# Two norms made one, and a value projection started before the head norms, in a 256-token transformer kernel

## The reference, cut to what matters

```python
def _rms(x, g):
    xf = x.astype(F32)
    y = xf * lax.rsqrt(jnp.mean(xf * xf, axis=-1, keepdims=True) + RMS_EPS)
    return (y * g.astype(F32)).astype(x.dtype)
...
return rmsnorm(x, final_g)                # end of first_block
...
h = x                                     # second_block
xn = _rms(h, norm_mix[i])
qa, ka, va, qb, kb, vb = jnp.split(xn @ w_in, [...], axis=-1)
oa = _moba(_rms(_heads(qa, MOBA_HEADS), qn_a), _rms(_heads(ka, MOBA_HEADS), kn_a), _heads(va, MOBA_HEADS), ...)
ob = _dilated(_rms(_heads(qb, DIL_HEADS), qn_b), _rms(_heads(kb, DIL_HEADS), kn_b), _heads(vb, DIL_HEADS), ...)
h = h + (concatenate([oa, ob]) @ w_out)
```

## Time and profile before

| what | us |
|---|---|
| median of 3 runs (lowest, highest) | 2900.24 (2899.81, 2912.12) |
| the profiled execution: its own time | 2900.88 |
| the profiled execution: span, first to last instruction | 2898.9 |
| TensorE matmul busy | 2687.6 (93%) |
| TensorE weight load busy | 2263.1 (78%) |
| VectorE busy | 1563.7 (54%) |
| ScalarE busy | 1320.6 (46%) |
| GpSimd busy | 22.0 (1%) |
| mean granted TensorE clock | 0.953 |

### The profile page before, as it was taken

How to read it: one execution, slowest core, us unless ns; L and a number is a source line. 1 busy time by engine, 2 the same in 40 slices (tenths; PEclk the granted TensorE clock), 3 DMA queues, 4 the chain that set the end, 5 groups by cost and what they waited for, 6 DMA issues and landing times. The chain is left out here.

```text
span 2898.9 us, 40646 instructions
## 1 busy us (share of the span) xinstructions
PE 2687.6 (93%) x15617; PEld 2263.1 (78%) x15617; DVE 1563.7 (54%) x2281; ACT 1320.6 (46%) x2001; POOL 22.0 (1%) x34
## 2 busy tenths in 40 slices
PE   6999998998899999899999798997899998889998
PEld 3788786875688877688876657997669997768998
DVE  7444434885644433644323565545757656556655
ACT  6444323464544422544312354544446544445644
POOL 0000000000000000000000000000000001000000
PEclk9999998999999999999999899999999999779999
DMA  6444532201344422344322202544215544302544
GB/s 244 174 159 163 191 138 73 97 20 44 119 170 153 165 102 101 122 168 155 131 90 100 103 1 81 181 174 162 102 59 188 181 178 162 128 11 73 188 174 145
DMA packets 52721, 374.81 MB, mean 129 GB/s; under 512 B 5823, under 2 KB 7035, under 8 KB 8737
## 3 DMA queue, kind: packets, MB, share of 16 engines
q1 hardware_dynamic: 50288, 360.73, 34.7%
q0 software_dynamic: 1920, 12.27, 1.2%
q10 hardware_dynamic: 432, 0.73, 0.1%
HBM read 372.55 MB, written 7.39 MB: 131 GB/s over the span
## 5 line engine op out<-in xcount | busy, mean ns | idle before, releaser
L1092 DVE TENSOR_TENSOR wlo<-raw,whi 128x1024 fp32r<-128x1024 f32 x666 | 799.6, 1222 | 823.0 <-ACT whi L657 821.9
L657 ACT ACTIVATE whi<-raw 128x1024 fp32r<-128x1024 f32 x666 | 684.7, 1053 | 867.6 <-PE acc L1586 781.5
L1584 PE MATMUL acc<-hhi,whi 128*128 128x256 f32 (+1 forms) x2800 | 939.7, 336 | 53.9 <-DVE hlo L1176 36.2
L1585 PE MATMUL acc<-hlo,whi 128*128 128x256 f32 (+1 forms) x2800 | 934.0, 334 | 0.0
L1586 PE MATMUL acc<-hhi,wlo 128*128 128x256 f32 (+1 forms) x2800 | 933.0, 333 | 0.0
L1584 PEld LDWEIGHTS acc<-hhi,whi 128*128 128x128 f32 x2800 | 536.4, 192 | 117.0 <-issue 61.9
L1586 PEld LDWEIGHTS acc<-hhi,wlo 128*128 128x128 f32 x2800 | 536.4, 192 | 50.8
L1585 PEld LDWEIGHTS acc<-hlo,whi 128*128 128x128 f32 x2800 | 536.8, 192 | 48.8 <-issue 0.2
L1584 PE MATMUL acc<-ghi,whi 128*128 128x512 f32 (+1 forms) x1056 | 364.0, 345 | 22.5 <-DVE glo L1249 15.1
L1585 PE MATMUL acc<-glo,whi 128*128 128x512 f32 (+1 forms) x1056 | 362.8, 344 | 0.0
L1586 PE MATMUL acc<-ghi,wlo 128*128 128x512 f32 (+1 forms) x1056 | 362.5, 343 | 0.0
(11 more groups left out here) (245 smaller groups left out, 2584.6 us busy)
## 6 DMA issues: line engine op xcount, KB each, us to landing
raw<-in_slabs SPq DMA_DIRECT2D x333, 1024.0 KB, 4.8
ada_raw<-in_slabs SPq DMA_DIRECT2D x8, 1024.0 KB, 22.8
skew_dram<-lines_dram POOLq DMA_DIRECT2D x1, 6144.0 KB, 24.9
bt<-skew_dram POOLq DMA_DIRECT2D x4, 1024.0 KB, 6.5
x<-in_x_in SPq DMA_DIRECT2D x1, 2048.0 KB, 18.0
out<-x SPq DMA_DIRECT2D x1, 1024.0 KB, 4.8
rope<-in_rope POOLq DMA_DIRECT2D x1, 512.0 KB, 4.0
mask<-in_mask POOLq DMA_DIRECT2D x1, 512.0 KB, 4.7
```

The source lines that it names most:

```text
L657: nc.scalar.activation(whi[:, n % 2, cols], raw_of(n, cols), ACT.Copy).then_inc(ready, 1)
L1092: nc.vector.tensor_tensor(wlo[:, n % 2, cols], raw_of(n, cols), whi[:, n % 2, cols].bitcast(F32), ALU.subtract).then_inc(low, 1)
L1584: nc.tensor.matmul(out, w[0], xx[0], start=first, stop=False)
L1585: nc.tensor.matmul(out, w[0], xx[1], start=False, stop=False)
```

## The change

Four things are changed, all between the last `down` of the first block and the end of the first decoder attention.

1. The final norm is no stage of its own. With `both` set, ScalarE squares each pair of tiles twice: once scaled by the root of eps (columns 0 to 255 of `sq`), once scaled by `final_g` (two instructions of 128x256, columns 256 to 511). VectorE's adds to `prod` are 128x1024 in place of 128x512. TensorE sums both parts into one bank in four matmuls, which gives the mean square of the normed stream times its norm, and then makes two more for the plain sum (`x_summed`). One root and one reciprocal give the scale of the mixer norm of the final norm, and `two_gains` holds the product of both gains. The loops over the halves of `down` are written out, and the root's table is loaded by `preload` behind the last `hi`.
2. `x` itself gets its final norm later: the second root goes to `rs[:, 256:512]` (`x_root`), VectorE takes its reciprocal in unit 11, and the eight products, each followed by a wait for itself, in units 12 to 19.
3. TensorE does value slab 0 and half of value slab 1 before it waits for `att_ready`; the other half stands behind the first three scores, and a wait for ScalarE's copy of slab 1 behind that. Slab 1 has a bank of its own, the one in which the units' transposes lie. Slabs 2 and 3 go, in 11 units each, into units 2 to 12 and 13 to 23, one and two steps in turn.
4. ScalarE's and VectorE's half-slabs stand elsewhere: `hi` of the first free slab ahead of the units and `lo` in units 0 and 2, the others `hi` in 4, 7, 14, 17, 25, 28 and `lo` in 5, 8, 15, 18, 26, 29. The copies of slabs 2 and 3 stand at the start of units 14 and 24.

```diff
@@ -166,9 +167,10 @@
             st += ffn_stages(1, S, mod=2)
-    st += [Stage("norm", T=S, how="final")]
+    st[-1].both = True
     for layer in range(2):
         st += [Stage("norm", T=S, how="gain", gain=VCOL["norm_mix"] + DT * layer)]
+        st[-1].both = layer == 0
         if layer == 0:
@@ -516,9 +522,17 @@
+def value_bank(c):
+
+    return acc[:, 1, 1, :] if c == 1 else v_bank
+
 def turn_bank(st, u):
...
     return acc[:, 1, 1, :] if st.what == "ab" else acc[:, u % 2, 1, :]
+
+def gain_of(st, c):
+
+    return two_gains[:, c:c + 1] if st.both else vec[:, st.gain + c:st.gain + c + 1]
@@ -593,6 +606,8 @@
         pool.wait_ge(rs_ready, st.rs0 + 1)
+        if st.both:
+            pool.wait_ge(x_summed, 1)
         for k in range(1, st.items, 2):
@@ -690,8 +705,12 @@
         act.wait_ge(sum_done, st.sum0 + (1 if st.summed else DT))
-        nc.scalar.activation(rs[:, 0:st.T], sums[:, 0:st.T], ACT.Sqrt, bias=eps[:, 0:1], scale=1.0 / D)\
-            .then_inc(std_ready, 1)
+        nc.scalar.activation(rs[:, 0:st.T], sums[:, 0:st.T], ACT.Sqrt,
+                             bias=(eps_sq if st.both else eps)[:, 0:1], scale=1.0 / D).then_inc(std_ready, 1)
+        if st.both:
+            act.wait_ge(x_summed, 1)
+            nc.scalar.activation(rs[:, S:2 * S], B[2][:, 0:S], ACT.Sqrt, bias=eps[:, 0:1],
+                                 scale=1.0 / (D * ROOT_EPS * ROOT_EPS)).then_inc(x_root, 1)
@@ -772,17 +791,22 @@
                         act.wait_ge(sq_added, st.add0 + c + 1 + 2 * i)
-                        nc.scalar.activation(sq[:, :, 0:st.T], x[:, bass.ds(2 * c + 4 * i, 2), 0:st.T],
-                                             ACT.Square).then_inc(sq_ready, 1)
+                        ins = nc.scalar.activation(sq[:, :, 0:st.T], x[:, bass.ds(2 * c + 4 * i, 2), 0:st.T],
+                                                   ACT.Square, scale=ROOT_EPS if st.both else 1.0)
+                        for t in range(2) if st.both else ():
+                            g = VCOL["final_g"] + 2 * c + t + 4 * i
+                            ins = nc.scalar.activation(sq[:, t, S:2 * S], x[:, 2 * c + t + 4 * i, 0:S],
+                                                       ACT.Square, scale=vec[:, g:g + 1])
+                        ins.then_inc(sq_ready, 1)
                     hi(st.n0 + 2 + ks * c + kk, i, 2 * ks)
-        if st.feeds:
+        if st.feeds or st.both:
             half(0)
...
                 half(i)
-        if st.feeds:
+        if st.feeds or st.both:
             preload(ACT.Sqrt)
@@ -796,8 +820,6 @@
             root(st)
-        if st.how == "final":
-            return
         for k in range(st.items):
@@ -1036,16 +1057,19 @@
             value_rows(0)
+            hi(st.n0 + 2)
         for u in range(LEAD):
             exps(u)
+        if ab:
+            value_rows(1)
         for u in range(UNITS):
-            if ab and u % 8 == 0 and u:
-                value_rows(u // 8)
+            if ab and u in (14, 24):
+                value_rows(2 + u // 24)
             copied(u)
...
                 exps(u + LEAD)
-            if ab and u % 8 in (2, 5):
-                hi(st.n0 + u // 8 + 2, halves=(u % 8 // 5,))
+            if ab and u in (4, 7, 14, 17, 25, 28):
+                hi(st.n0 + 3 + u // 10, halves=((u % 10 + u // 20) // 7,))
             if u % 4 == 1 and u > 4:
@@ -1255,8 +1278,9 @@
+        wide = 2 * S if st.both else st.T
         dve.wait_ge(g_lo, st.g0 + 1)
-        step.done(nc.vector.memset(prod[:, :, 0:st.T], 0.0))
+        step.done(nc.vector.memset(prod[:, :, 0:wide], 0.0))
         if st.kind == "pw2":
@@ -1296,11 +1320,11 @@
                         dve.wait_ge(sq_added, st.add0 + c + 1 + 2 * i)
-                        nc.vector.tensor_tensor(prod[:, :, 0:st.T], prod[:, :, 0:st.T], sq[:, :, 0:st.T],
+                        nc.vector.tensor_tensor(prod[:, :, 0:wide], prod[:, :, 0:wide], sq[:, :, 0:wide],
                                                 ALU.add).then_inc(sq_added, 1)
...
-        if st.feeds:
+        if st.feeds or st.both:
             half(0)
@@ -1542,8 +1566,17 @@
                 biased(u + LEAD)
-            if st.what == "ab" and u % 8 in (3, 6):
-                lo(st.n0 + u // 8 + 2, halves=(u % 8 // 6,))
+            if st.what == "ab" and u == 11:
+                dve.wait_ge(x_root, 1)
+                step.done(nc.vector.reciprocal(rs[:, S:2 * S], rs[:, S:2 * S]))
+            if st.what == "ab" and 12 <= u < 20:
+                c, g = u - 12, VCOL["final_g"] + u - 12
+                step.done(nc.vector.scalar_tensor_tensor(x[:, c, 0:S], x[:, c, 0:S], vec[:, g:g + 1],
+                                                         rs[:, S:2 * S], ALU.mult, ALU.mult))
+            if st.what == "ab" and u in (0, 2):
+                lo(st.n0 + 2, halves=(u // 2,))
+            if st.what == "ab" and u in (5, 8, 15, 18, 26, 29):
+                lo(st.n0 + 3 + u // 10, halves=((u % 10 + u // 20) // 8,))
             if u % 4 == 2 and u > 4:
@@ -1675,6 +1708,17 @@
         pe.wait_ge(sq_added, st.add0 + 1)
+        if st.both:
+            for c in range(2):
+                nc.tensor.matmul(sums[:, 0:S], ones, prod[:, c, S:2 * S], start=(c == 0), stop=False)
+            for c in range(2):
+                ins = nc.tensor.matmul(sums[:, 0:S], ones, prod[:, c, 0:S], start=False,
+                                       stop=(c == 1))
+            ins.then_inc(sum_done, 1)
+            for c in range(2):
+                ins = nc.tensor.matmul(B[2][:, 0:S], ones, prod[:, c, 0:S], start=(c == 0), stop=(c == 1))
+            ins.then_inc(x_summed, 1)
+            return
         for c in range(2):
@@ -1884,8 +1928,8 @@
         x_final(pe, st)
-        pe.wait_ge(att_ready, st.att0 + 1)
         if st.what != "ab":
+            pe.wait_ge(att_ready, st.att0 + 1)
             pe.wait_ge(kd_dve, 2 if nsa else 1)
@@ -1900,11 +1944,14 @@
                 slab_there(n)
-                if c:
-                    pe.wait_ge(acc_free[(st.m0 + c - 1) % 2], freed(st.m0 + c - 1))
+                last = st.m0 + (0 if c == 2 else 2)
+                if c < 2:
+                    set_free(st.m0 + c)
+                else:
+                    pe.wait_ge(acc_free[last % 2], freed(last))
             if step == 8:
                 second_half(n)
-            o = v_bank[:, S * tt:S * tt + S]
+            o = value_bank(c)[:, S * tt:S * tt + S]
             a, rows = k * SLAB_N, slice(P * tt, P * tt + P)
@@ -1918,6 +1965,9 @@
                 value_step(0, step)
+            for step in range(8):
+                value_step(1, step)
+            pe.wait_ge(att_ready, st.att0 + 1)
@@ -1972,15 +2022,20 @@
             scores(u)
+        if ab:
+            for step in range(8, 16):
+                value_step(1, step)
+            pe.wait_ge(acc_free[(st.m0 + 1) % 2], freed(st.m0 + 1))
         for u in range(UNITS):
...
                 values(u - 1)
-            if ab and u < 24:
-                value_step(1 + u // 8, 2 * (u % 8))
-                value_step(1 + u // 8, 2 * (u % 8) + 1)
+            if ab and 2 <= u < 24:
+                c, j = 2 + (u - 2) // 11, (u - 2) % 11
+                for step in range((16 * j + 5) // 11, (16 * j + 21) // 11):
+                    value_step(c, step)
         values(UNITS - 1)
```

34 lines of the change are left out of this document (18 added, 16 removed).

## The result

The changed kernel is slower: 2917.46 us median of 20 runs (2912.54 to 2935.01), against 2901.01 for the kernel before beside it; the ratio is 1.0046, with a 95% interval of 1.0028 to 1.0063. The profiled execution took 2918.06 us, 17.2 more than the one of before, with a mean granted clock of 0.939 against 0.953. Of the forecast cases it is the one with chance 0.03.

The account below looks back on a forecast made before the run. TensorE was taken as nearly always busy except around the norms and the wait for head norms. 10.0 + 5.3 + 0.6 - 0.2 = 15.7 us gained, a median of 2884.5 us; 8 of 10 within 2879 to 2891.

Parts of the forecast that it names:

- The step that failed: Units of the first decoder attention: new waits priced at their own length, such as +1.5 us in unit 13.
- The units: First decoder attention's units: +7.0 against -7.75 us, 0.6 gained with small overlaps; last eight units -0.2.
- unit 0's `lo`: Unit 0 has no value step to hide VectorE's `lo` of 1.13 us: 2.32 against 0.67, +1.65 us.
- unit 13: TensorE waits there for value bank 0, which ScalarE frees only behind slab 2's copy: +1.5 us.
- the gap before `att_ready`: Attention front: 2.4 us of TensorE idling remain; if the clock falls there, 1.5 us are lost again.
- The rival that happened: *Slower*: with a third of the value steps gone, the units run at clock 0.50: 2924 us, chance 0.03.
- The first 24 units: First decoder attention, 24 units: 53.5 us, or about 93 at clock 0.50 under the slower rival.
- Norms, -10.0: Final and mixer norms before the projection: one root and hidden table load start the projection 10.0 us earlier.
- ScalarE's table load: Norms: the root's 1.28 us load goes behind `hi` and is hidden; no extra drain counted.
- Front, -5.3: Attention front: early value slabs bring the first transpose 5.1 us after the first scores, 5.3 us gained.
- VectorE's prices: Units 12 to 19: each product of `x` 0.41 us, 0.6 with its wait for itself.
- `down`, 0: Last `down`: extra squares and adds cost nothing, with 0.15 us to spare before `wlo` half-slabs are needed.

Follow-up runs that it names:

- e4_lo_ahead: The changed kernel with both halves of `lo` of value slab 2 put ahead of unit 0 on VectorE: 2901.2 us.
- e7_copy_early: e4_lo_ahead with ScalarE's copy of value slab 2 ahead of unit 13's copy, in place of unit 14: 2889.5 us.
- e12_lo_last: e9_pool with both halves of `lo` of slab n0+5 moved from units 26 and 29 behind the last unit: 2871.35 us, ratio 0.9881.
- e1_norm_only: The changed kernel with its fused norm kept and the old order of value slabs taken back: 2928.7 us.
- e10_stall_burst: e6_one_stall with 40 unread filler matmuls of 128x256 added in unit 9: ten runs within 2912.5 to 2914.5 us.
- e6_one_stall: The kernel before with one 128x512 reciprocal put into VectorE's queue in unit 4: 2937.0 to 2940.6 us in four runs.
- e5_norm_fill: e1_norm_only with 20 unread matmuls in the 2.15 us wait for the first softmax: 2890.4 us.
- e9_pool: Changed kernel with slab 2's `lo` and copy earlier, steps over units 0 to 23, fillers, `x` products on GpSimd, reciprocal in quarters: 2883.1 us, ratio 0.9918.

## Why the prediction was wrong

- **The step that failed** is the sentence that a stall costs its own length: every wait in "The units" was priced so (+1.65 for unit 0's `lo`, +1.5 for unit 13), and the clock only for the gap before `att_ready` (1.5 us). The sizes were right (1.64 and, at full clock, 1.34 us), the cost was not: the first lost the clock for 100 us, and e4_lo_ahead without it was 16 us faster. Without the second wait as well, e7_copy_early was 12 us faster again.
- **The rival that happened** had its time nearly right (2924 against 2917.5) and its mechanism wrong. Units with fewer steps do hold 1.00, as e12_lo_last shows with the same 32 steps, and units with all steps stay at 0.50 once it is lost (e1_norm_only, e10_stall_burst). What it needed was a wait at the entry. The prediction had that wait on its list, at unit 0, and did not bring the two together. The argument against it, the second decoder attention at 1.00, rested on one window, 2606 to 2616 us. The same attention stands at 0.50 until 2572, which shows a clock regained there, and nothing of units 0 to 28 of the first.
- **A sign that was passed over.** The trace of the kernel before has the mechanism in small: 1.02 us of waiting ahead of unit 28, and the clock at 0.50 from 2152.3 to 2155.6. The prediction read the units at 1.00 from a window that ends at 2130.
- **The first 24 units** took 81.8 us (transposes 2076.62 to 2158.45) against 53.5 forecast and 93 for the rival.
- **Norms, -10.0: right.** From the last addition to `x` to the projection's first matmul 12.30 us against 12.4; sums at half clock (2.07, 1.91 and 1.91 us for the three rows of four), root to projection 4.75 against 4.76. The rest of the 11.1 is the last addition, which came 0.99 us earlier. No term foresaw that, and no run shows it to be the change's doing: between the profiled runs that moment differs by up to 5.9 us.
- **ScalarE's table load:** hidden. Its row is 1.28 us here too and the spare operation behind it starts 0.01 us after it ends, so the drain that the Trainium skill (ScalarE: Activation LUTs, What ACT_TABLE_LOAD costs) adds is again in no row.
- **Front, -5.3: 3.6 came.** First transpose 6.77 us after the first scores against 5.1. The clock fell at 2070.6 behind the 2.15 us of idling (forecast 2.4) and was back at 2074: the 1.5 us that the text named and left out of the sum.
- **VectorE's prices:** the product takes 0.47 and the next operation starts 0.51 after it (2116.12 to 2116.63), against 0.6 priced and 0.41 without a wait. The Trainium skill (VectorE: DVE Perf Modes, The DRAIN you can't avoid) has a semaphore after each operation cost nothing extra; the trace gives 0.10 at most, between that rule and the 0.19 that was taken.
- **`down`, 0:** right; no new wait for `wlo`, the last addition came earlier, not later.

## What to carry to other kernels

In a stage in which TensorE's work comes in small pieces, price a new wait by what the clock loses behind it, up to where comparable rows show it back, not by its length, and look for such waits first at the entry, where the pipeline fills. If a kernel's runs fall into groups with different mean clocks, look for one gap ahead of such a stage; filling it with unread matmuls costs a few microseconds and shows at once whether a group hangs on it. Then remove the waits by moving work of the feeding engine to an idle engine or behind the last unit, and keep the fillers only where a wait is certain.

## What the runs showed of the hardware

- The granted clock has a memory. The same code kept 1.00 (e10_stall_burst from 2124 to 2160 us) or 0.50 (from 2104 to 2122) by what lay ahead of it. The Trainium skill (TensorE: Matmul & The Clock Gate, HAM oscillation — how this bites in real kernels) describes waits between bursts that lower the clock again and again; the traces agree on the fall, and add a stage in which it lasts: units 0 to 28 raised it in no profile, in the changed kernel not in 88 us of them with TensorE occupied nearly throughout.
- When it rises differs. Value slab 0 had it 3.0 us after its start, the fillers of e10_stall_burst 3.2 us, `wo` between 2.8 us (e1_norm_only) and 6.2 us (the changed kernel). Matmuls without a pause are no warrant for it: from 2509 to 2529 us the kernel before runs 96 of 128x64 one behind the other (L1584 to L1586), and all of them have 0.50.
- The same wait of 2.15 us, with the same rows around it, kept the clock in the kernel before and in e10_stall_burst and lost it in e1_norm_only and e6_one_stall. The wait of 1.02 us ahead of unit 28 lost it within half a microsecond in the kernel before, and in e5_norm_fill the clock stayed 1.00 over it and fell only at 2147.1, 1.1 us after the end of one of 2.03 us that follows. What decides was not settled. The Trainium skill (TensorE: Matmul & The Clock Gate, Part 1: The HAM clock gate) says that the monitor does not start with the kernel, so that the moment of a change varies; the two outcomes agree with that and do not prove it.
- While GpSimd worked on `x` in e9_pool, some of VectorE's small rows were longer: a normalising of 128x128, 0.29 us elsewhere, took 0.85 and 0.65.

```profile
2096.38 5.59 POOL L625 TENSOR_TENSOR x<-x,rs 128x256 f32<-128x256 f32 x8 [85.98 <-DVE rs L1589]
```
```profile
2096.35 0.85 DVE L1570 TENSOR_SCALAR sc<-sc,stt 128x128 f32<-128x128 f32 x1
...
2104.31 0.65 DVE L1570 TENSOR_SCALAR sc<-sc,stt 128x128 f32<-128x128 f32 x1
2109.20 0.29 DVE L1570 TENSOR_SCALAR sc<-sc,stt 128x128 f32<-128x128 f32 x1
```
